# First pair of attention scores, maxima and exponentials moved ahead of the last projection unit, in a two-layer hybrid backbone on one core

## The reference

```python
for l in range(2):
    hx = rms_norm(x, norm1_g[l]) * (1 + sc1) + sh1       # hc: the same for the context
    b, c, xx, u, q_g, k_g, v_g, q_w, k_w, v_w = split_proj(hx @ w_in[l])
    q, k = apply_rope(rms_norm(heads(q), qn)), apply_rope(rms_norm(heads(k), kn))   # no rope on context
    y_a = b * dwconv(c * xx, conv_a_w[l])                # 3 taps
    g = dwconv(u[..., :256] * sigmoid(u[..., 256:]), conv_b_w[l]) + conv_b_b[l]     # 31 taps
    y_b = silu(layer_norm(g))
    o_g = softmax(q_g @ [k_g, kc_g].T / 8) @ [v_g, vc_g]             # 4 heads on 2 key heads
    o_w = softmax(q_w @ [window of k_w, kc_w].T / 8, sink) @ ...     # 4 heads on 2 key heads
    x = x + g1 * (concat([y_a, y_b, o_g, o_w]) @ w_out[l])
    x = x + g2 * hier_moe(rms_norm(x, norm2_g[l]) * (1 + sc2) + sh2) # 32 experts, 2 per token
```

## Time and profile before

| what | value |
|---|---|
| median of three runs | 1848.68 us (1841.0 to 1850.56) |
| profiled execution | 1849.2 us, span 1847.6 us |
| PE busy | 1621.6 us, 88% of the span |
| DVE, ACT, POOL busy | 35%, 17%, 12% |
| chain that ended last | PE 63%, DMA 27%, DVE 7%, ACT 2% |
| mean granted TensorE clock | 0.957 of full speed |

### The profile page before, as it was taken

How to read it: one execution, slowest core, us unless ns; L and a number is a source line. 1 busy time by engine, 2 the same in 40 slices (tenths; PEclk the granted TensorE clock), 3 DMA queues, 4 the chain that set the end, 5 groups by cost and what they waited for, 6 DMA issues and landing times.

```text
span 1847.6 us, 27090 instructions
## 1 busy us (share of the span) xinstructions
PE 1621.6 (88%) x9896; PEld 942.9 (51%) x9897; DVE 647.8 (35%) x1643; ACT 310.9 (17%) x709; POOL 219.7 (12%) x346
## 2 busy tenths in 40 slices
PE   5999998999779899999796899899879979787784
PEld 3555445744456556665453444575446546344442
DVE  2094645533722222222122776552531111111113
ACT  4111115731200000000000411372300000000000
POOL 0000000000012122222111000000012112111111
PEclk9999999999879999999999899999979999999997
DMA  9358146021569999899998702302479999999995
GB/s 386 168 207 369 67 205 277 5 69 68 203 266 426 427 424 426 339 425 426 427 425 340 301 0 96 132 1 75 181 292 426 425 426 425 426 427 425 427 425 205
DMA packets 55001, 530.67 MB, mean 287 GB/s; under 512 B 12056, under 2 KB 12728, under 8 KB 25504
## 3 DMA queue, kind: packets, MB, share of 16 engines
q1 hardware_dynamic: 37760, 492.26, 63.7%
q0 software_dynamic: 14432, 27.15, 3.9%
q10 hardware_dynamic: 2752, 10.49, 1.5%
HBM read 520.85 MB, written 26.28 MB: 296 GB/s over the span
## 4 chain that ended last, share of the span: by engine, by line
PE 63%; DMA 27%; DVE 7%; ACT 2%; issue 1%; ACTq 0%; SPq 0%; POOLq 0%; DVEq 0%
PE ps L932 24%; DMA ring<-in_e_down_dram 13%; DMA ring<-in_e_up_dram 11%; PE ps L655 10%; PE ps L688 7%; PE ps L878 5%; PE ps L734 3%; PE ps L782 3%; PE ps L605 3%; PE ps L803 2%; DMA r<-y_dram 1%; PE ps L920 1%; PE ps L969 1%; DVE r L1531 1%; PE ps L627 1%
## 5 line engine op out<-in xcount | busy, mean ns | idle before, releaser
L932 PE MATMUL ps<-ring,r 128*64 128x256 f32 (+1 forms) x3888 | 535.7, 431 | 71.9 <-DMA ring<-in_e_up_dram 34.4
L932 PEld LDWEIGHTS ps<-ring,r 128*64 128x64 f32 x3888 | 312.1, 139 | 279.9 <-issue 132.2
L932 PE MATMUL ps<-r 128*64 128x256 f32 (+1 forms) x1768 | 241.0, 425 | 30.9 <-DMA r<-in_e_up_dram 14.8
L1528 DVE TENSOR_TENSOR r<-r,ps 128x128 f32<-128x128 f32 x142 | 34.4, 284 | 541.6 <-PE ps L932 541.6
L932 PEld LDWEIGHTS ps<-r 128*64 128x64 f32 x1768 | 142.5, 138 | 121.3 <-issue 54.5
L655 PE MATMUL ps<-r,ring 128*128 128x512 f32 (+1 forms) x480 | 177.9, 530 | 3.7 <-ACT r L1671 2.1
L688 PE MATMUL ps<-ring,r 128*128 128x512 f32 (+1 forms) x384 | 158.4, 567 | 0.0
L878 PE MATMUL ps<-ring,r 128*128 128x512 f32 x320 | 142.9, 603 | 0.8 <-DVE r L1324 0.8
L655 PEld LDWEIGHTS ps<-r,ring 128*128 128x128 f32 x480 | 91.2, 192 | 91.9 <-issue 81.2
L1548 DVE TENSOR_TENSOR r<-ps,r 128x512 f32<-128x512 f32 x71 | 49.1, 692 | 211.2 <-PE ps L932 211.2
L1838 ACT ACTIVATE r<-ps 128x256 f32<-128x256 f32 x71 | 27.2, 383 | 548.2 <-PE ps L932 548.2
(11 more groups left out here) (217 smaller groups left out, 1305.0 us busy)
## 6 DMA issues: line engine op xcount, KB each, us to landing
ring<-in_e_up_dram SPq DMA_DIRECT2D x44, 2048.0 KB, 35.1
ring<-in_e_down_dram SPq DMA_DIRECT2D x44, 2048.0 KB, 35.4
ring<-in_e_gate_dram SPq DMA_DIRECT2D x43, 2048.0 KB, 32.6
ring<-in_w_mod_dram SPq DMA_DIRECT2D x24, 2048.0 KB, 17.7
r<-in_e_gate_dram SPq DMA_DIRECT2D x20, 2048.0 KB, 35.9
r<-in_e_up_dram SPq DMA_DIRECT2D x20, 2048.0 KB, 38.2
r<-in_e_down_dram SPq DMA_DIRECT2D x20, 2048.0 KB, 38.4
ring<-in_w_in_dram SPq DMA_DIRECT2D x8, 2048.0 KB, 20.2
```

The lines of the kernel that those rows point to most:

```text
L932: mm = pe.matmul(ps[g * B:(g + 1) * B, bank, 0:width], x, w[:, k, g * width:(g + 1) * width], start=(k == first), stop=(k == last), tile_p ...
```

## The change

`first_scores` is cut out of PE's `attention` and called ahead of the projection of unit 11, the last one. DVE takes both maxima of pair 0 in the turn of unit 10, behind its rotation and ahead of its `store_qk`; before, they stood in the turn of unit 11 on both sides of its rotation. ACT takes both exponentials of pair 0 ahead of `qkv_copies` of unit 11; before, they stood behind it. In the first iteration of the attention loop PE turns head 0 ahead of the scores of pair 1. The layer norm's steps are tied to one unit earlier (`LN_MEAN`, `LN_VAR`), one more tap stands ahead of the units, and the table of mod chunks puts two chunks beside the ninth conv tile and none beside units 10 and 11; so chunks 13 to 23 move forward by one step, and the two chunks of `w_in` for the units move back by one place in the ring's order. The number of chunks and their slots for the experts stay.

```diff
     mod = [("mod", n) for n in range(12 * DEPTH)]
     steps, mod = mod[:MOD_FIRST], mod[MOD_FIRST:]
     for n, step in enumerate(conv + qkv):
-        beside = 2 if n == 9 else 0 if n in (14, 15, 21) else 1
+        beside = 2 if n in (8, 9) else 0 if n in (14, 15, 20, 21) else 1
         steps += [step, *mod[:beside]]
         mod = mod[beside:]
     return steps
...
 
 
         H1_BY_VECTOR, H1_BY_SCALAR = (0, 2, 4, 6, 7), (1, 3, 5)
-        LN_MEAN, LN_VAR = 7, 9
-        TAPS_EARLY = 24
+        LN_MEAN, LN_VAR = 6, 8
+        TAPS_EARLY = 25
         CONV_ACT = {ct: n + 1 for n, ct in enumerate(CONV_ORDER[:8])}
         CONV_MUL = {4: 1, 5: 2}
         CONV_AT = {ct: n for n, ct in enumerate(CONV_ORDER)}
...
                                        tile_position=(0, kv * HD))
                 mm.then_inc(o_psum[layer], 1)
 
-            def attention(layer):
-                units = units_of(layer)
-                pairs = len(units) // 2
+            def first_scores(layer):
                 pe.wait_ge(qkT_ready, QKV_UNITS * layer + NT)
                 pe.wait_ge(ln_centred, 3 * layer + 3)
                 if layer == 0:
                     pe.wait_ge(mod_ready, 3)
                     pe.wait_ge(mod_rows, 12 * DEPTH)
-                scores(layer, 0, units)
+                scores(layer, 0, units_of(layer))
+            def attention(layer):
+                units = units_of(layer)
+                pairs = len(units) // 2
                 pe.wait_ge(qkT_ready, QKV_UNITS * layer + QKV_UNITS - 1)
                 for pair in range(pairs):
-                    if pair + 1 < pairs:
-                        scores(layer, pair + 1, units)
-                    attend(layer, 2 * pair, units[2 * pair])
+                    if pair == 0:
+                        attend(layer, 0, units[0])
+                        scores(layer, 1, units)
+                    else:
+                        if pair + 1 < pairs:
+                            scores(layer, pair + 1, units)
+                        attend(layer, 2 * pair, units[2 * pair])
                     if pair == 0:
                         qk_transposes(layer, QKV_UNITS - 1)
                     else:
...
                     if kind == "qkv":
                         if layer and n < QKV_AHEAD:
                             h1_transposes(layer, 2 * n, 2 * n + 2)
+                        if n == QKV_UNITS - 1:
+                            first_scores(layer)
                         qkv_projection(layer, n)
                         if n in (LN_MEAN, LN_VAR):
                             ln_sums(layer, 0 if n == LN_MEAN else 1)
...
                         mod_copy(1, MOD_CONV - 12, 4, turned_bank(MOD_CONV), len(MOD_TURNED))
                     if layer == 0 or u >= QKV_AHEAD:
                         square_sums(layer, u)
-                        if u == QKV_UNITS - 1:
-                            unit_max(layer, 0, units_of(layer)[0])
                         rotate(layer, u)
-                        if u == QKV_UNITS - 1:
-                            unit_max(layer, 1, units_of(layer)[1])
                     if TAPS_EARLY + u < TAPS_B:
                         conv_b_tap(layer, TAPS_EARLY + u)
                     if u == LN_VAR + 1:
                         ln_scale(layer)
+                    if u == QKV_UNITS - 2:
+                        for v in range(2):
+                            unit_max(layer, v, units_of(layer)[v])
                     if u < QKV_UNITS - 1:
                         store_qk(layer, u)
                     if u == LN_MEAN:
...
 
             def attention(layer):
                 units = units_of(layer)
-                ac.wait_ge(rows_in, 32)
                 ac.wait_ge(qkv_psum, QKV_UNITS * layer + QKV_UNITS)
-                for u in (0, 1):
-                    unit_exp(layer, u, units[u])
                 for u in range(0, len(units), 2):
                     for v in (u, u + 1):
                         unit_pT(layer, v, units[v])
...
                     if kind == "conv" and n in CONV_ACT:
                         conv_copies(layer, [n])
                     if kind == "qkv":
+                        if n == QKV_UNITS - 1:
+                            ac.wait_ge(rows_in, 32)
+                            ac.wait_ge(qkv_psum, QKV_UNITS * layer + n)
+                            for u in range(2):
+                                unit_exp(layer, u, units_of(layer)[u])
                         qkv_copies(layer, n)
                         if n == LN_MEAN + 1:
                             ln_squares(layer)
```

## The result

| | before | after |
|---|---|---|
| median, us (runs on one chip, side by side) | 1847.93 (19 runs, 1840.97 to 1852.07) | 1851.82 (19 runs, 1846.25 to 1857.10) |
| ratio | | 1.0029 [1.0017, 1.0042] |
| profiled execution: time, span, mean clock | 1849.2, 1847.6, 0.957 | 1849.45, 1847.7, 0.955 |
| ACT busy, instructions | 310.9, x709 | 315.6, x713 |

The changed kernel is slower by about 5 us (3.1 to 7.8 by the interval), which is less than 0.5%. 1853 was forecast. The two profiled executions differ by 0.25 us only: executions of one program lie up to 11 us apart here, so single spans don't show a change of 5 us, and I compare stretch by stretch.

The account below looks back on a forecast made before the run. PE was taken to bound attention and DMA of weights the experts. First layer -0.4, second layer +4.0 and clock +0.9 gave +4.5 us on 1849.2, 1853 for a median; range 1845 to 1859 us.

Parts of the forecast that it names:

- Second layer, +4.9 forecast: Second layer's attention entry: pair 2 4.0 us later by waits, plus 0.9 us for the low clock.
- The queue: Second layer: exponentials queued on ACT hold up unit 11's square root, then DVE and PE; pair 2 begins 4.0 us later.
- The clock: Second layer: longer PE holes let the low clock catch the scores of pair 1; +0.9 us, between 0 and +2.
- First layer, -0.4 forecast: First layer's attention entry, reordering waits included: -0.4 us, between -2.5 and +1.5.
- the early exponentials buy little: First layer: scores of pair 1 release what follows, behind a unit 11 moved back by 1.6 us; pair 2 at 299.7 against 300.19.
- The reordering, +0.55 forecast: First layer, ahead of the entry: moved mod chunks add 0.70 us of wait and save 0.15; nothing in the second layer.
- The 0.70: First layer, ninth conv tile: one more turning follows its chunk at once and waits 0.70 us for ACT's copy.
- Both entries keep the full clock: Rival, both attention entries: turnings between the holes shorten them, saving about 2 us in each entry; 1848.5 us, chance 0.2.
- Tables cost more than I hide: Rival, both layers: the load ahead of head 2's exponential waits for maxima, 1.28 us each, +2.6; 1856 us, chance 0.14.
- The low clock stays: Rival, second layer: longer holes leave PE low for two pairs more, 6 us on top of 4.5; 1860 us, chance 0.06.
- The experts moved with attention, one for one: Experts behind attention in both layers: what is lost or won at attention's entry reaches the end one for one.

Follow-up runs that it names:

- behind_first: Changed kernel with, in the first layer alone, exponentials behind unit 11's copies and scores of pair 1 ahead of turning head 0: 1847.02 us, 0.9997 of before.
- clock_held: Changed kernel with matmuls of constants, computing nothing used, put in PE's holes at both entries: 1844.81 us, 0.9993 of before.
- second_only: Changed kernel with the moved entry in the second layer alone, the first entering as before: 1849.62 us, 1.0015 of before.
- after_again: The changed kernel, unaltered, profiled a second time: single execution 1856.81 us.
- first_only: Changed kernel with the moved entry in the first layer alone, the second entering as before: 1845.92 us, 0.9992 of before.
- behind_second: Changed kernel with, in the second layer alone, exponentials behind unit 11's copies and scores of pair 1 ahead of turning head 0: 1841.46 us, 0.9975 of before.
- neither: Changed kernel with the old entry in both layers, keeping moved mod chunks, earlier layer norm and tap: 1844.18 us, 0.9987 of before.
- exps_after: Changed kernel with, in both layers, exponentials behind unit 11's copies and scores of pair 1 ahead of turning head 0: 1838.99 us, 0.9953 of before.
- exps_after_fill: exps_after with two matmuls of constants ahead of the scores of pair 1 in both layers: 1839.42 us, 0.9963 of before.
- before_again: The kernel before, unaltered, profiled a second time: single execution 1839.96 us.

## Why the prediction was right

**Second layer, +4.9 forecast (4.0 by the queue, 0.9 by the clock).** Measured: the mean of four profiles of the new entry (153.1 with behind_first's 153.15) against the two of before (148.2) gives +4.9. The mechanism is the one forecast, but that the sums agree so closely is luck: one part was smaller, one much larger, and a third, which was not forecast, went against it. The parts can be told apart with clock_held, whose rows run at the full clock from unit 11 on.

- *The queue.* At the full clock pair 3 begins at 85.66 in clock_held. In before it begins at 82.0 in both profiles when the slow rows between pairs 2 and 3 are taken back to 4.75 us (84.30 - 2.28, 82.78 - 0.77); the context unit that the last section shows ran at the low clock in all three. That is +3.65 for the forecast's 4.0. Pair 2, ahead of the slow rows of before, says the same (80.91 against 77.27). The chain is the one forecast: scaling of the layer norm late, exponentials 4 us behind unit 11, its root behind them, and DVE and PE behind that.
- *The clock.* Pair 3 comes 2.9 us behind 85.66 in second_only and in behind_first (88.53). In the two profiles of after the slow rows cost 4.35, 1.36 in the scores of pair 1 and 2.98 between pairs 2 and 3. The mean is 3.6 against 1.5 in before: +2.1. This is the mis-sized term: 0.9 counted the scores of pair 1 alone, and not that the low level then lasts on through the work of pair 2.
- *What came against it.* In the two profiles of after one context unit far ahead of the entry ran at the full clock, 1.69 us less (the last section has the rows), in the two others not: -0.85 in the mean. The prediction has no such term.

**First layer, -0.4 forecast** (its steps add up to -0.5), which is -1.0 without the 0.55 of the reordering ahead of the entry. From the end of unit 11 to pair 3 before took 18.15 and 18.50 us. The new entry, with 1.57 added for the scores of pair 0, which now lie ahead of that end, took 14.72 in after, 17.58 in after_again, 17.75 in first_only and 17.60 in behind_second, so -1.4 in the mean, -3.6 where the clock held, -0.7 where it did not. Against neither and second_only, which have the old entry in the new order (16.74 both), it is +0.2. The steps themselves came within 0.3 us; the early exponentials buy little, as forecast, since the scores of pair 1 release what follows. The order of exps_after takes 14.2 to 14.7 in all four profiles (exps_after twice, exps_after_fill, behind_first).

**The reordering, +0.55 forecast within that -0.4,** is the step that the runs don't bear out as a sum. The 0.70 was there (at 172.55 in after, for ACT's mod row), yet neither came out at 0.9987 [0.9974, 1.0001]. In its first layer pair 3 is 1.4 to 1.8 us earlier than in before: the low clock came sooner (0.50 from 294 to 298), some 2.5 us of it in holes, and the scores of pair 2 take 1.45 us, where before has 2.49. In the second layer the reordering was put at nothing, but one new wait takes 1.36 us of PE, for DVE's gains on unit 10, in a place where before has no wait. At the full clock that is 1.3 us at pair 3 (83.31 against 82.0); the low level that before has there did not come in neither or first_only, which pays for it. The first two rows are neither's first layer, the third its second:

```profile
291.99 1.87 PE L735 MATMUL ps<-r 64*128 64x256 f32 x12 [2.10 <-DVE r L1243]
...
300.02 1.45 PE L735 MATMUL ps<-r 64*128 64x256 f32 x8
...
1180.56 0.33 PE L672 MATMUL ps<-const,r 128*128 128x128 f32 x1 [1.36 <-DVE r L1251]
```

**The rivals.** *Both entries keep the full clock* came true for the first layer in one of four profiles, never for the second. *Tables cost more than I hide* is refuted by the rows at 290.33 and 1187.18: each load ends 2.87 and 3.80 us ahead of its exponential. *The low clock stays* is refuted by the window of 1200: the full clock is back by pair 3. The low level did last longer than in before, as that rival feared, but the cost is the +2.1 above, not 6. The experts moved with attention, one for one: 464.1 us from start to end in before's second layer, 464.6 in after's.

**What stays open.** exps_after is 0.76% below after by the two ratios (about 14 us, some 3.5 either way), where these stretches give 2.3 in the first layer and 5.8 in the second. The rest must lie where both programs are the same. The profiles differ there too: the first output projection took 95.2 and 95.0 us in after, 92.6 in both of exps_after, and the stretch ahead of the second layer's conv tiles 44.1 and 44.2 against 42.1 and 42.2. The output projection's excess does not come with after's first layer as such: first_only and behind_second, where that layer is the same program, took 92.6. Why the other stretch should be shorter was not tested. So the better order is shown to be faster, but only some 8 of its 14 us are traced to the entries.

## What to carry to other kernels

Work that is put ahead on an in-order engine "under cover" delays all that is queued behind it: measure the cover in each layer (unit 11 takes 7.1 us in one, 3.7 in the other), and ask what is due when the cover ends. Here the better edit puts the moved exponentials behind the late unit's short copies on ACT, and the turning that needs them behind the scores of pair 1 on PE; ACT's half alone gave less. Where holes of PE can't be closed, price the slow rows behind them as well: here these cost 3.6 us beside the 3.65 of the queue, and a few matmuls of constants took them back.

## What the hardware showed that I had not expected

The same rows behind the same hole run at either clock level. The second context unit of the second layer (unit 5) follows a wait of 2.11 us; PE in after, then in exps_after, whose second layer is the same program up to there:

```profile
1132.65 0.44 PE L670 MATMUL ps<-const,r 128*128 128x128 f32 x2 [2.11 <-DVE r L1266]
...
1133.03 3.62 PE L688 MATMUL ps<-ring,r 128*128 128x256 f32 x16
```

```profile
1129.10 0.44 PE L670 MATMUL ps<-const,r 128*128 128x128 f32 x2 [2.11 <-DVE r L1262]
...
1129.48 5.31 PE L688 MATMUL ps<-ring,r 128*128 128x256 f32 x16
```

The unit takes 3.62 us in one (clock 1.00 from 1132 to 1138) and 5.31 in the other (0.50 from 1131 to 1133). At this place two profiles of one program agreed each time (3.62 twice in after, 5.31 twice in before and in exps_after), so the level here could hang on the program. Elsewhere one program shows both: the first entry of after took 3 us more in one execution than in the other, and in the first layer the chunk behind the layer norm's sums of squares (L605) took 3.61 us in before (0.50 from 268 to 270) and 1.92 in before_again, 1.92 in after and 3.52 in after_again. A handful of such places, each worth 1.5 to 3 us and falling one way or the other, could account for most of the 11 us between executions of one program; what decides it no run here shows.
